# Layer norms of the second block by halves on three engines, and the bias table copied from DRAM to DRAM

## The chip, the cores and the metric

The kernel runs on one core of a Trainium2 chip. The metric is the device time of one execution in microseconds, the median over several runs. The five engines are named as the profile names them: PE is TensorE (PEld its weight loads), DVE is VectorE, ACT is ScalarE, POOL is GpSimd, SP is SyncE; SPq and ACTq are the DMA queues that SyncE and ScalarE issue into.

## What is computed

Two layers of one kind (`first_block`: a feed-forward block, a mixer, a second feed-forward block), then one layer of another kind on 256 tokens of 1024 channels in float32. The last layer is:

```
def layer_norm(x, g, b):
    xf = x.astype(jnp.float32)
    mu = xf.mean(-1, keepdims=True)
    var = jnp.square(xf - mu).mean(-1, keepdims=True)
    return ((xf - mu) * lax.rsqrt(var + LN_EPS)).astype(x.dtype) * g + b

def hybrid_layer(...):
    h = x @ w_in
    ...
    attn = moba_attention(to_heads(q), to_heads(k), to_heads(v), rel_bias)
    ...
    mix = jnp.concatenate([attn, conv, pool], axis=-1) @ w_out
    x = layer_norm(DEEPNORM_ALPHA * x + mix, ln1_g, ln1_b)
    up = causal_dwconv(x @ w_up, ffn_conv_w) + ffn_conv_b
    u, g = jnp.split(up, 2, axis=-1)
    ff = (u * jax.nn.silu(g)) @ w_down
    return layer_norm(DEEPNORM_ALPHA * x + ff, ln2_g, ln2_b)
```

The attention of that layer adds a bias that depends on the distance of query and key alone: `tab[t5_bucket(rel)]` for 8 heads.

## The kernel before

The 256 tokens lie as two tiles of 128 (`x[:, t, :]`, t = 0 and 1, 1024 channels each); `HALVES` names the four pieces of 512 channels, (0,0), (0,1), (1,0), (1,1). Every engine has its program written out by hand in its own order, and semaphores (`S[...]`) tie them together. Float32 products are made of three passes with a high and a low part: weights come by DMA of 1 MB from SyncE (`fill`, L461) into six slots, ScalarE writes the high part (`act_high`, L433, the copy itself L437), VectorE the low part (`dve_low`, L439, L442), and a slot is filled again when both have read it. So a late load shows as a wait of ScalarE for the DMA, then of VectorE for ScalarE, then of TensorE for VectorE.

A feed-forward block (`pe_ffn`, `act_ffn`, `dve_ffn`) runs over 11 groups of 256 hidden channels: groups 0 and 1 written out, 2 to 9 in a loop, 10 written out. There are four of them in layers 0 and 1 (f = 0 and 1 in each), all with the same work; once a group VectorE writes `ff_lo` (L670). The bias table: early in the kernel TensorE makes one row of 384 values per head, and VectorE puts it in `spread` (8 partitions x 384). For the attention, query row p needs the row shifted by p, so the row is first written 128 times to `scratch` in DRAM, and `bias2` is then loaded from there with one element less per partition (L2075, issued by SyncE in the second block's program behind `sp.wait_ge(spread_out, 32)`). The writing is `act_bias_out` (L366), called at the end of groups 0 and 1 of the last feed-forward block of layer 1 (L654): four heads each time, 4 x 128 rows of 1536 B read from four partitions of `spread`:

```
act.dma_start(scratch.ap().rearrange("p h x -> h p x")[at],
              spread[at].unsqueeze(1).broadcast_to([4, P, 384])).then_inc(spread_out, 16)
```

The layer norms of the second block are in `dve_ln` (L1914), run twice (n = 0 behind the output projection, n = 1 at the end of the kernel). TensorE gives the four pieces of the sum in order ("half_done" for the first three, "used" for the last). VectorE adds the residual in two pieces (L1923), takes the statistics (L1928, L1930), subtracts the mean and multiplies by the gain over all 1024 channels (L1936), and scales by the reciprocal root and adds the bias (L1942). ScalarE makes the root (`act_ln`, L1907). Tile 0 and tile 1 are interleaved on VectorE: `residual(0), stats(0), centred(0), residual(1), scaled(0), stats(1), centred(1), scaled(1)`. Behind norm 0, TensorE transposes x, eight times a tile (`pe_turn`, L738), and ScalarE (L767) and VectorE (L775) write the high and low parts of the transposed x in four pieces; the first matmul of the next block waits for the third. ScalarE loads the gains and biases of norm 1 into `ln_gb` when norm 0 is done (L1874). Behind norm 1, ScalarE issues one store per token tile (L1904).

## Time and profile before

| | us |
|---|---|
| median of 3 runs | 1517.83 (1517.06 to 1518.89) |
| profiled execution, its own time | 1520.03 |
| its span in the profile | 1518.0 |
| TensorE (PE) busy | 1415.2 (93%) |
| VectorE (DVE) busy | 941.1 (62%) |
| ScalarE (ACT) busy | 716.9 (47%) |
| GpSimd (POOL) busy | 179.7 (12%) |

Busy times of engines overlap. The mean granted clock of TensorE is 0.964 of full speed, and 230.53 MB went over the DMA queues, 152 GB/s over the span. All starts are in us from the span's start.

### The profile page before, as it was taken

To read this page: it belongs to the slowest core of one execution; us is meant where nothing else is said; L and a number is where in the kernel's file an instruction comes from. 1 tells how busy PE (TensorE), PEld (TensorE's weight loads), DVE (VectorE), ACT (ScalarE), POOL (GpSimd) and SP (SyncE) were. 2 spreads that over 40 slices of the span, in tenths; PEclk is the share of its full clock that TensorE was granted. 3 is DMA by queue.
4 is the path that set the end of the run, shared out by engine and by line. 5 is a ranking of instruction groups with operands and counts; after the bars stand their busy time and mean duration, and the time that the engine had idled before them with its cause. 6 is when DMAs were issued, how large, how long until landed. Compare 5 with 4: busy or idle time off the path is not lost.

```text
span 1518.0 us, 25173 instructions
## 1 busy us (share of the span) xinstructions
PE 1415.2 (93%) x10017; PEld 1238.2 (82%) x10017; DVE 941.1 (62%) x1246; ACT 716.9 (47%) x1010; POOL 179.7 (12%) x177
## 2 busy tenths in 40 slices
PE   6999999998899999999999998896999989799995
PEld 5888889887788887888889877785888967789995
DVE  5665567666666556666666665654566554577666
ACT  6444465444644446444466444633444334344442
POOL 3000000495000000000000495000000041000000
PEclk9999999999999999999999999998999988799998
DMA  9655373101665544655373100757644720755530
GB/s 327 222 193 180 102 242 105 57 3 40 218 217 191 192 151 156 222 179 182 115 229 119 57 3 28 229 124 208 211 139 138 241 113 30 241 174 168 202 100 28
DMA packets 173163, 230.53 MB, mean 152 GB/s; under 512 B 4576, under 2 KB 154752, under 8 KB 172958
## 3 DMA queue, kind: packets, MB, share of 16 engines
q1 hardware_dynamic: 169664, 222.71, 44.4%
q10 hardware_dynamic: 2813, 6.62, 1.7%
q8 instruction: 55, 0.90, 0.2%
q0 software_dynamic: 608, 0.12, 0.0%
q14 instruction: 23, 0.18, 0.0%
HBM read 226.81 MB, written 2.62 MB: 151 GB/s over the span
## 4 chain that ended last, share of the span: by engine, by line
PE 74%; POOL 10%; DVE 7%; DMA 4%; ACT 3%; issue 2%; SPq 1%; ACTq 0%; DVEq 0%; POOLq 0%
PE bank L457 41%; PE bank L555 20%; PE bank L556 10%; POOL mix L1698 5%; POOL proj L1696 4%; DMA w_up<-in_ffn_w_up_dram 3%; DVE hT L775 1%; DVE up_lo L442 1%; DVE gate_lo L442 1%; DMA w_gate<-in_ffn_w_gate_dram 1%; PE bank L1004 1%; PE bank L1047 0%; SPq L467 0%; DVE x L710 0%; ACT up_hi L437 0%
## 5 line engine op out<-in xcount | busy, mean ns | idle before, releaser
L555 PE MATMUL bank<-hT,gate_hi 128*128 128x512 f32 x704 | 259.7, 409 | 15.6 <-DVE gate_lo L442 10.0
L555 PE MATMUL bank<-hT,up_hi 128*128 128x512 f32 x704 | 252.1, 400 | 7.6 <-DVE up_lo L442 7.6
L442 DVE TENSOR_TENSOR down_lo<-w_down,down_hi 128x2048 fp32r<-128x2048 f32 x67 | 153.5, 2291 | 99.5 <-ACT down_hi L437 99.5
L442 DVE TENSOR_TENSOR gate_lo<-w_gate,gate_hi 128x2048 fp32r<-128x2048 f32 x67 | 153.5, 2290 | 81.4 <-ACT gate_hi L437 81.3
L556 PE MATMUL bank<-hT,gate_lo 128*128 128x256 f32 x704 | 201.6, 286 | 0.0
L635 ACT ACTIVATE work<-bank 128x256 f32<-128x256 f32 x176 | 66.7, 383 | 279.3 <-PE bank L556 279.3
L556 PE MATMUL bank<-hT,up_lo 128*128 128x256 f32 x704 | 198.3, 282 | 0.0
L442 DVE TENSOR_TENSOR up_lo<-w_up,up_hi 128x2048 fp32r<-128x2048 f32 x72 | 162.6, 2258 | 48.8 <-ACT up_hi L437 48.7
L437 ACT ACTIVATE down_hi<-w_down 128x2048 fp32r<-128x2048 f32 x67 | 128.3, 1916 | 109.1 <-PE bank L457 105.7
L555 PEld LDWEIGHTS bank<-hT,gate_hi 128*128 128x128 f32 x704 | 137.1, 195 | 51.6 <-issue 18.1
L555 PEld LDWEIGHTS bank<-hT,up_hi 128*128 128x128 f32 x704 | 132.9, 189 | 42.0 <-DVE up_lo L442 5.4
L437 ACT ACTIVATE up_hi<-w_up 128x2048 fp32r<-128x2048 f32 x72 | 136.5, 1896 | 58.3 <-PE bank L457 44.7
L457 PE MATMUL bank<-down_hi,ff_hi 128*128 128x512 f32 x400 | 157.8, 394 | 3.3 <-DVE down_lo L442 3.3
L457 PE MATMUL bank<-down_hi,ff_lo 128*128 128x512 f32 x400 | 156.9, 392 | 0.0
L457 PE MATMUL bank<-down_lo,ff_hi 128*128 128x512 f32 x400 | 156.6, 392 | 0.0
L679 DVE TENSOR_TENSOR work<-bank,work 128x256 f32<-128x256 f32 x176 | 73.6, 422 | 130.8 <-ACT work L635 130.8
L457 PE MATMUL bank<-hT,up_hi 128*128 128x256 f32 x768 | 144.6, 290 | 3.9 <-DVE hT L775 3.9
L437 ACT ACTIVATE gate_hi<-w_gate 128x2048 fp32r<-128x2048 f32 x67 | 128.3, 1915 | 35.6 <-PE bank L457 17.2
L556 PEld LDWEIGHTS bank<-hT,gate_lo 128*128 128x128 f32 x704 | 137.9, 196 | 1.4
L556 PEld LDWEIGHTS bank<-hT,up_lo 128*128 128x128 f32 x704 | 133.8, 190 | 0.0
L457 PEld LDWEIGHTS bank<-hT,up_hi 128*128 128x128 f32 x768 | 123.3, 198 | 6.1 <-issue 5.3
L457 PE MATMUL bank<-hT,gate_hi 128*128 128x256 f32 x608 | 113.3, 288 | 1.5 <-DVE hT L775 1.5
(322 smaller groups left out, 2422.5 us busy)
## 6 DMA issues: line engine op xcount, KB each, us to landing
w_gate<-in_ffn_w_gate_dram SPq DMA_DIRECT2D x44, 1024.0 KB, 5.4
w_up<-in_ffn_w_up_dram SPq DMA_DIRECT2D x44, 1024.0 KB, 5.4
w_down<-in_ffn_w_down_dram SPq DMA_DIRECT2D x44, 1024.0 KB, 5.0
w_up<-in_w_in_dram SPq DMA_DIRECT2D x12, 1024.0 KB, 11.0
w_down<-in_w_in_dram SPq DMA_DIRECT2D x12, 1024.0 KB, 8.4
w_gate<-in_w_up_dram SPq DMA_DIRECT2D x11, 1024.0 KB, 6.0
w_up<-in_w_up_dram SPq DMA_DIRECT2D x11, 1024.0 KB, 5.2
w_down<-in_w_down_dram SPq DMA_DIRECT2D x11, 1024.0 KB, 5.0
```

The source lines that it names most:

```text
L437: act.activation(staged[kind][0][:, 0:cols], slot[sl][:, 0:cols], ACT.Copy).then_inc(high[sl], 1)
L442: dve.tensor_tensor(staged[kind][1][:, 0:cols], slot[sl][:, 0:cols], staged[kind][0][:, 0:cols].bitcast(F32), ALU.subtract).then_inc(split ...
L457: mm = pe.matmul(out_, lhs(l_), rhs(r_), start=first and i == 0, stop=last and i == 2, **kw)
L555: pe.matmul(bank[:, :], w[0][:, c, at], hpair[:, :, c, :], start=c == 0, stop=False)
L556: mm = pe.matmul(bank[:, 0:SEQ], w[1][:, c, at], hT[0][:, c, :], start=False, stop=c == KC - 1)
L635: act.activation(low[:, q, j * SEQ:(j + 1) * SEQ], psum[2 * q + j][:, SEQ:], ACT.Copy)\
L679: dve.tensor_tensor(whole[:, q, at], psum[2 * q + j][:, 0:SEQ], low[:, q, at], ALU.add)\
L775: dve.scalar_tensor_tensor(hT[1][:, c:c + step, t * P:(t + 1) * P], turned_bank(t, c, step), col(gain, c) if gain else 1.0, hT[0][:, c:c + ...
L1004: mm = pe.matmul(out_[:, 6 * t:6 * t + 6], src(c, t), const("pick")[:, 10 - 2 * c:16 - 2 * c], start=(c == 0), stop=(c == 2))
L1696: link(pool.tensor_tensor(part[:, :, lag:], z[:, :, 0:n], per_channel("conv_dw_w", CONV_W - 1 - lag, n), mult))
L1698: ins = pool.tensor_tensor(acc[:, :, lag:], acc[:, :, lag:], part[:, :, lag:], add)
```

## The change

1. The bias table. `act_bias_row` writes the 8 x 384 values once to a new DRAM tensor `bias_row` (12 KB), in group 1 of the first feed-forward block. Four DMAs then copy this row of 3072 values 32 times each into `scratch`, from DRAM to DRAM; ScalarE issues them in groups 0 and 1 of the second feed-forward block of layer 0 and of the first one of layer 1. SyncE waits for 64 instead of 32.
2. The layer norms. VectorE takes each half through residual and statistics as it comes. Tile 0 is then normalised by ScalarE (one pass a half, with reciprocal root as scale and minus mean times it as bias) and finished by GpSimd (times gain, plus bias, a half at a time). Tile 1 stays on VectorE, the last step in halves.
3. TensorE transposes a half as soon as it is ready (`pe_turned_ln`), and the output is stored in four halves.

```
+        bias_row = nc.dram_tensor("bias_row", [NH2, 384], F32)
+        def act_bias_row(act):
+            act.wait_ge(spread_ready, 1)
+            act.dma_start(bias_row.ap(), spread).then_inc(row_out, 16)
...
         def act_bias_out(act, part):
             if part == 0:
-                act.wait_ge(spread_ready, 1)
-            at = slice(4 * part, 4 * part + 4)
-            act.dma_start(scratch.ap().rearrange("p h x -> h p x")[at],
-                          spread[at].unsqueeze(1).broadcast_to([4, P, 384])).then_inc(spread_out, 16)
+                act.wait_ge(row_out, 16)
+            row = bass.AP(bias_row, 0, [[0, 32], [1, NH2 * 384]])
+            act.dma_start(scratch.ap()[32 * part:32 * part + 32].rearrange("p h x -> p (h x)"), row)\
+               .then_inc(spread_out, 16)
...
-                if (uses.layer, f) == (DEPTH - 1, 1) and isinstance(g, int) and g < 2:
-                    act_bias_out(act, g)
+                if uses.layer + f == 0 and isinstance(g, int) and g == 1:
+                    act_bias_row(act)
+                if uses.layer + f == 1 and isinstance(g, int) and g < 2:
+                    act_bias_out(act, 2 * uses.layer + g)
...
+        def pe_turned_ln(pe):
+            for t, h in HALVES:
+                pe.wait_ge(S[("ln_pooled", "normed")[t]], h + 1 + past[("ln_pooled", "normed")[t]])
+                for c in range(4):
+                    mm = pe.transpose(psum[4 + 2 * t + h][:, c * P:(c + 1) * P],
+                                      x[:, t, h * 512 + c * P:h * 512 + (c + 1) * P], ident)
+                mm.then_inc(S["turned"], 1)
...
-            pe_turn(pe, 1, x, "normed", count=0)
+            pe_turned_ln(pe)
...
-            act.wait_ge(S["normed"], NT + past["normed"])
+            act.wait_ge(S["ln_pooled"], 2 + past["ln_pooled"])
+            act.wait_ge(S["normed"], 2 + past["normed"])
...
-            for t in range(NT):
-                act.wait_ge(S["normed"], NT + t + 1 + past["normed"])
-                act.dma_start(out[0, t * P:(t + 1) * P, :], x[:, t, :]).then_inc(stored, 16)
-            act.wait_ge(stored, 16 * NT)
+            for t, h in HALVES:
+                act.wait_ge(S[("ln_pooled", "normed")[t]], 2 + h + 1 + past[("ln_pooled", "normed")[t]])
+                act.dma_start(out[0, t * P:(t + 1) * P, h * 512:(h + 1) * 512], x[:, t, h * 512:(h + 1) * 512])\
+                   .then_inc(stored, 16)
+            act.wait_ge(stored, 16 * len(HALVES))
...
+                if t == 0:
+                    act.wait_ge(S["ln_factors"], n + 1 + past["ln_factors"])
+                    for h in range(2):
+                        xs = x[:, 0, h * 512:(h + 1) * 512]
+                        act.activation(xs, xs, ACT.Identity, bias=lnbias[:, 0:1], scale=rstd[:, 4:5])\
+                           .then_inc(S["ln_flat"], 1)
+
+        def pool_ln(pool, n):
+            pool.wait_ge(x_in, 16 * (1 + 2 * n + 2))
+            for h in range(2):
+                at = slice(h * 512, (h + 1) * 512)
+                pool.wait_ge(S["ln_flat"], 2 * n + h + 1 + past["ln_flat"])
+                pool.tensor_tensor(x[:, 0, at], x[:, 0, at], ln_gb[:, 0, at], ALU.mult).then_inc(S["ln_scaled"], 1)
+                pool.wait_ge(S["ln_scaled"], 2 * n + h + 1 + past["ln_scaled"])
+                pool.tensor_tensor(x[:, 0, at], x[:, 0, at], ln_gb[:, 1, at], ALU.add).then_inc(S["ln_pooled"], 1)
...
+            half_in(0, 0)
+            half_in(0, 1)
+            half_in(1, 0)
+            dve.wait_ge(S["rms_root"], NT * n + 1 + past["rms_root"])
+            link(dve.reciprocal(rstd[:, 4:5], rstd[:, 0:1]))
+            dve.scalar_tensor_tensor(lnbias[:, 0:1], lnvar[:, 0, 0:1], -1.0, rstd[:, 4:5], ALU.mult, ALU.mult)\
+               .then_inc(S["ln_factors"], 1)
+            half_in(1, 1)
+            dve.wait_ge(x_in, 16 * (1 + 2 * n + 2))
+            link(dve.scalar_tensor_tensor(x[:, 1, :], x[:, 1, :], lnvar[:, 1, 0:1], ln_gb[:, 0, :],
+                                          ALU.subtract, ALU.mult))
+            dve.wait_ge(S["rms_root"], NT * n + 2 + past["rms_root"])
+            link(dve.reciprocal(rstd[:, 5:6], rstd[:, 1:2]))
+            for h in range(2):
+                at = slice(h * 512, (h + 1) * 512)
+                dve.scalar_tensor_tensor(x[:, 1, at], x[:, 1, at], rstd[:, 5:6], ln_gb[:, 1, at],
                                          ALU.mult, ALU.add).then_inc(S["normed"], 1)
...
-            sp.wait_ge(spread_out, 32)
+            sp.wait_ge(spread_out, 64)
```

`half_in(t, h)` is residual and statistics of one half (and the aggregate behind the second half of a tile), each step waiting for the one before. Line numbers behind the change are a few higher than before.

ScalarE's order at the bias copies, before, in group 0 of the last feed-forward block of layer 1 (`hot` holds `spread`; the sizes are those of the destination):

```order
L648 ACT_TABLE_LOAD
L648 ACTIVATE work<-work 128x512
L437 ACTIVATE up_hi<-w_up 128x2048
L437 ACTIVATE down_hi<-w_down 128x2048
L371 DMA bias_scratch<-hot 4x128x384
L635 ACTIVATE work<-bank 128x256 x2
L437 ACTIVATE gate_hi<-w_gate 128x2048
```

And after, in group 0 of the second feed-forward block of layer 0:

```order
L655 ACT_TABLE_LOAD
L655 ACTIVATE work<-work 128x512
L444 ACTIVATE up_hi<-w_up 128x2048
L444 ACTIVATE down_hi<-w_down 128x2048
L378 DMA bias_scratch<-bias_row 32x3072
L642 ACTIVATE work<-bank 128x256 x2
L444 ACTIVATE gate_hi<-w_gate 128x2048
```

The copy has the same place in a group, now in two other blocks, and its outer dimension is 32 where it was 4.

VectorE's order in the first of the two norms, before:

```order
L1923 SCALAR_TENSOR_TENSOR x<-x,bank 128x512 x2
L1928 BN_STATS small<-x 128x6 x2
L1930 BN_AGGR small<-small 128x2
L1936 SCALAR_TENSOR_TENSOR x<-x,small,work 128x1024
L1923 SCALAR_TENSOR_TENSOR x<-x,bank 128x512 x2
L1941 RECIPROCAL small<-small 128x1
L1942 SCALAR_TENSOR_TENSOR x<-x,small,work 128x1024
L1928 BN_STATS small<-x 128x6 x2
L1930 BN_AGGR small<-small 128x2
L1936 SCALAR_TENSOR_TENSOR x<-x,small,work 128x1024
L1941 RECIPROCAL small<-small 128x1
L1942 SCALAR_TENSOR_TENSOR x<-x,small,work 128x1024
```

And after, from the third half on (`work` is the gain and bias, `bank` the sum in PSUM):

```order
L1956 SCALAR_TENSOR_TENSOR x<-x,bank 128x512
L1957 BN_STATS small<-x 128x6
L1967 RECIPROCAL small<-small 128x1
L1968 SCALAR_TENSOR_TENSOR small<-small 128x1
L1956 SCALAR_TENSOR_TENSOR x<-x,bank 128x512
L1957 BN_STATS small<-x 128x6
L1960 BN_AGGR small<-small 128x2
L1972 SCALAR_TENSOR_TENSOR x<-x,small,work 128x1024
L1975 RECIPROCAL small<-small 128x1
L1978 SCALAR_TENSOR_TENSOR x<-x,small,work 128x512 x2
```

Two of the four passes over 1024 channels with `work` as input are gone from VectorE. What they did stands at the end of GpSimd's program, for both norms behind its last step of the pooling:

```order
L2081 TENSOR_TENSOR work<-work,proj 128x512
L1944 TENSOR_TENSOR x<-x,work 128x512
L1946 TENSOR_TENSOR x<-x,work 128x512
L1944 TENSOR_TENSOR x<-x,work 128x512
L1946 TENSOR_TENSOR x<-x,work 128x512
```

The four operations on x come once for each norm, after ScalarE's two passes L1936.

## Rows read from the trace of the kernel before

**Rows 1.** The page, part 4: the chain that ended last, by engine

```profile
PE 74%; POOL 10%; DVE 7%; DMA 4%; ACT 3%; issue 2%; SPq 1%; ACTq 0%; DVEq 0%; POOLq 0%
```

**Rows 2.** Line L670, last blocks of layer 0, layer 1: min/median/max ns, starts

```profile
L670 DVE TENSOR_TENSOR ff_lo<-work,ff_hi x10: 692/693/694, 411.9 to 557.5; 128x512 fp32r<-128x512 f32 x10
...
L670 DVE TENSOR_TENSOR ff_lo<-work,ff_hi x10: 691/693/694, 982.8 to 1145.5; 128x512 fp32r<-128x512 f32 x10
```

**Rows 3.** Waits of TensorE, 930 to 1200 us: total us, times, longest

```profile
PE bank L555 <- DVE gate_lo L442: 10.0, 1, 10.0
PE bank L555 <- DVE up_lo L442: 4.6, 3, 2.1
```

**Rows 4.** Timeline of SyncE's queue and ScalarE: start us, duration us

```profile
407.53 0.37 SPq L467 DMA_DIRECT2D w_gate<-in_ffn_w_gate_dram  x1
...
997.85 20.04 SPq L467 DMA_DIRECT2D w_up<-in_ffn_w_up_dram  x1
...
414.68 1.93 ACT L437 ACTIVATE gate_hi<-w_gate 128x2048 fp32r<-128x2048 f32 x1
```

**Rows 5.** Windows, last block of layer 1; last columns: TensorE clock, DMA share, GB/s

```profile
1003.00:1006.00 3.00, 3.00 (x19) 2.58 (x18) 1.42 (x2) 2.36 (x3) 0.00 (x0) 1.00 0.25 41
...
1036.00:1039.00 3.00, 0.00 (x0) 0.00 (x0) 0.00 (x0) 1.10 (x1) 0.00 (x0) 0.50 0.26 38
```

**Rows 6.** DMA issues: page part 6 (KB, us to landing); the bias load L2075

```profile
w_gate<-in_ffn_w_gate_dram SPq DMA_DIRECT2D x44, 1024.0 KB, 5.4
...
L2075 SPq DMA_DIRECT2D work<-bias_scratch x1: 1534/1534/1534, 1191.0 to 1191.0; - x1
```

**Rows 7.** Timeline around the first norm: start us, duration us

```profile
1279.39 0.63 ACT L856 ACTIVATE hT<-mix 128x512 fp32r<-128x512 f32 x1
...
1290.80 1.28 DVE L1923 SCALAR_TENSOR_TENSOR x<-x,bank 128x512 f32<-128x512 f32 x2
...
1292.12 1.29 DVE L1928 BATCH_NORM_STATS2 small<-x 128x6 f32<-128x512 f32 x2
1293.44 0.21 DVE L1930 BATCH_NORM_AGGREGATE small<-small 128x2 f32<-128x12 f32 x1
...
1295.41 0.28 ACT L1911 ACTIVATE small<-small 128x1 f32<-128x1 f32 x1
1296.32 0.16 DVE L1941 RECIPROCAL small<-small 128x1 f32<-128x1 f32 x1
...
1300.80 1.29 DVE L1942 SCALAR_TENSOR_TENSOR x<-x,small,work 128x1024 f32<-128x1024 f32 x1
...
1302.14 1.97 PE L746 MATMUL bank<-cst,x 128*128 128x128 f32 x8 [2.31 <-DVE x L1942]
...
1305.65 0.77 PE L457 MATMUL bank<-hT,gate_hi 128*128 128x256 f32 x2 [1.54 <-DVE hT L775]
...
1311.93 0.40 PE L457 MATMUL bank<-hT,gate_hi 128*128 128x256 f32 x2
```

**Rows 8.** Timeline where GpSimd and VectorE work on SBUF at once

```profile
285.67 1.23 POOL L1684 TENSOR_TENSOR proj<-proj 128x512 f32<-128x512 f32 x1 [272.89 <-ACT proj L1397]
...
914.78 3.05 POOL L1696 TENSOR_TENSOR proj<-proj,par 128x464 f32<-128x464 f32 x1
...
919.26 0.95 POOL L1696 TENSOR_TENSOR proj<-proj,par 128x462 f32<-128x462 f32 x1
...
914.72 2.29 DVE L442 TENSOR_TENSOR down_lo<-w_down,down_hi 128x2048 fp32r<-128x2048 f32 x1 [0.31 <-ACT down_hi L437]
...
903.12 2.71 DVE L1626 TENSOR_TENSOR work<-work,cst 128x384 f32<-128x384 f32 x2
```

**Rows 9.** The second norm: timeline of VectorE, and the stores L1904

```profile
1504.22 0.69 DVE L1923 SCALAR_TENSOR_TENSOR x<-x,bank 128x512 f32<-128x512 f32 x1 [0.74 <-PE bank L457]
...
1513.63 1.28 DVE L1942 SCALAR_TENSOR_TENSOR x<-x,small,work 128x1024 f32<-128x1024 f32 x1
...
L1904 ACTq DMA_DIRECT2D out_dram<-x x2: 344/344/345, 1512.1 to 1514.9; - x2
```

More of the change, by code:

```diff
@@ L176 @@
     "cl_ready": 1, "mixc_ready": 2, "pool_ready": 0, "pool_mm": 0, "taps_act": 0, "taps_picked": 0, "lag_done": 0,
-    "taps_done": 0, "stats_ready": 0,
+    "taps_done": 0, "stats_ready": 0, "ln_factors": 0, "ln_flat": 0, "ln_scaled": 0, "ln_pooled": 0,
 }
@@ L208, in build @@
         spread_out = ctx.enter_context(nc.semaphore("spread_out"))
+        row_out = ctx.enter_context(nc.semaphore("row_out"))
         bias_in = ctx.enter_context(nc.semaphore("bias_in"))
@@ L223, in build @@
             mixa_ready conv_sig conv_acc cl_mean cl_sq cl_var cl_root cl_ready mixc_ready
-            pool_ready pool_mm taps_act taps_picked lag_done taps_done stats_ready""".split()
+            pool_ready pool_mm taps_act taps_picked lag_done taps_done stats_ready ln_factors ln_flat ln_scaled ln_pooled""".split()
         S = {n: ctx.enter_context(nc.semaphore(n)) for n in names}
@@ L1912, in act_ln @@
                    .then_inc(S["rms_root"], 1)
-        def dve_ln(dve, uses, kind, n, link):
-            def residual(t):
-                for h in range(2):
-                    if (t, h) != HALVES[-1]:
-                        dve.wait_ge(S["half_done"], 3 * n + 2 * t + h + 1 + past["half_done"])
-                    else:
-                        products_done(dve, uses, kind, -1)
-                    xs = x[:, t, h * 512:(h + 1) * 512]
-                    ins = dve.scalar_tensor_tensor(xs, xs, ALPHA, psum[4 + 2 * t + h][:, :], ALU.mult, ALU.add)
-                link(ins)
-            def stats(t):
-                for h in range(2):
-                    ins = dve.bn_stats(lnstat[:, h, :], x[:, t, h * 512:(h + 1) * 512])
-                link(ins)
-                dve.bn_aggr(lnvar[:, t, :], lnstat).then_inc(S["stats_ready"], 1)
-                dve.wait_ge(S["stats_ready"], NT * n + t + 1 + past["stats_ready"])
-            def centred(t):
-                if t == 0:
-                    dve.wait_ge(x_in, 16 * (1 + 2 * n + 2))
-                link(dve.scalar_tensor_tensor(x[:, t, :], x[:, t, :], lnvar[:, t, 0:1], ln_gb[:, 0, :],
-                                              ALU.subtract, ALU.mult))
-            def scaled(t):
-                dve.wait_ge(S["rms_root"], NT * n + t + 1 + past["rms_root"])
-                link(dve.reciprocal(rstd[:, 4 + t:5 + t], rstd[:, t:t + 1]))
-                dve.scalar_tensor_tensor(x[:, t, :], x[:, t, :], rstd[:, 4 + t:5 + t], ln_gb[:, 1, :],
-                                         ALU.mult, ALU.add).then_inc(S["normed"], 1)
-            residual(0)
-            stats(0)
-            centred(0)
-            residual(1)
-            scaled(0)
-            stats(1)
-            centred(1)
-            scaled(1)
@@ new lines, in dve_ln, with half_in @@
+        def dve_ln(dve, uses, kind, n, link):
+            def half_in(t, h):
+                if (t, h) != HALVES[-1]:
+                    dve.wait_ge(S["half_done"], 3 * n + 2 * t + h + 1 + past["half_done"])
+                else:
+                    products_done(dve, uses, kind, -1)
+                xs = x[:, t, h * 512:(h + 1) * 512]
+                link(dve.scalar_tensor_tensor(xs, xs, ALPHA, psum[4 + 2 * t + h][:, :], ALU.mult, ALU.add))
+                ins = dve.bn_stats(lnstat[:, h, :], xs)
+                if h == 1:
+                    link(ins)
+                    dve.bn_aggr(lnvar[:, t, :], lnstat).then_inc(S["stats_ready"], 1)
+                    dve.wait_ge(S["stats_ready"], NT * n + t + 1 + past["stats_ready"])
+            half_in(0, 0)
[14 more added lines that the diff above has]
+                dve.scalar_tensor_tensor(x[:, 1, at], x[:, 1, at], rstd[:, 5:6], ln_gb[:, 1, at],
+                                         ALU.mult, ALU.add).then_inc(S["normed"], 1)
@@ L2054, in pool_second @@
             pool.tensor_tensor(u, v, p_, ALU.subtract).then_inc(S["pool_ready"], 1)
+            pool_ln(pool, 0)
+            pool_ln(pool, 1)
         @block.sync
```

## Prediction

> **What bounds the kernel now.** I read the page first. TensorE carries 74% of the chain that ended last [rows 1], so a change pays only where TensorE stands still, or where it makes TensorE wait anew. The change touches three stretches of time: a feed-forward block whose first two groups also issue the bias copies, and the two layer norms of the second block.
>
> First the copies. A plain comparison sizes them. All feed-forward blocks of layers 0 and 1 do the same work, and VectorE's write of ff_lo (L670) comes once a group. Its ten occurrences span 411.9 to 557.5 us in layer 0, which is 145.6 us, and 982.8 to 1145.5 us in layer 1, which is 162.7 us [rows 2]. Both runs of ten start before a stall can act, so the last block loses **17.1 us**. The waits of TensorE name the place: one of 10.0 us for gate_lo and three of 4.6 us together for up_lo [rows 3]. Behind those stands a weight load, and the issue rows show why. SyncE hung in one issue for 20.04 us from 997.85, where an issue takes 0.37 us in layer 0 [rows 4]. The window rows tell what kept the queues busy: from 1003 to 1006 the DMA engines are busy for 0.25 of their time at 41 GB/s, and from 1036 to 1039 still for 0.26 at 38 GB/s, with TensorE idle and its granted clock at 0.50, the 1.2 GHz level [rows 5]. A quarter of 16 engines is four, and the copy has four outer rows. The other twelve engines idle, but a weight load is whole only when its share on the four slow ones has landed. The return to 2.4 GHz after that pause lies inside the 17.1 us.
>
> **The change, part by part.** *The old copies go.* Their 17.1 us go with them: in that block nothing else delays TensorE, as the twin block shows. What is late next there is what is late in layer 0, the usual low_copied and silu steps, which are in the 145.6 us already.
>
> *Four new copies come*, of 32 rows of 12,288 B (393 KB) each, in groups 0 and 1 of the two feed-forward blocks before. No row shows a transfer from DRAM to DRAM, so I bound it. Above: the old copy ran at 41 GB/s over four engines, 10 GB/s each; 393 KB over 16 engines is 24.6 KB each, 2.4 us. Below: nothing. The cover is the time between a load's landing and its use: in layer 0's group 0 a gate load is issued at 407.53, such a load lands in 5.4 us, and ScalarE takes it up at 414.68 [rows 4, 6], 1.75 us later than it could. Beyond that cover each copy costs at most 2.4 - 1.75 = 0.65 us, 2.6 us for four. I take **+0.3 us**, near the lower end, since TensorE is not ScalarE and stands further behind. Their issues, and that of the 12 KB row copy in the first block, stand in ScalarE's program between work that waits for TensorE anyway; at the 0.37 us of an issue they hide there, and without that wait each would cost its 0.37. The wait of SyncE for 64 instead of 32 stands ahead of the bias load at 1191.0 us [rows 6], more than 500 us behind the last copy, so neither it nor the loads behind it move.
>
> *The layer norms.* Before, VectorE does all of it. In the first one it starts at 1290.80, ends at 1302.09 (1300.80 + 1.29), and TensorE's first matmul of the next block starts at 1305.65 [rows 7]. After, VectorE takes each half as it comes: 0.68 us for the residual and 0.68 for the statistics, with two gaps of 0.02, is 1.41 us a half. Three halves and one aggregate (0.24) end at 1295.27. ScalarE's root is there at 1295.69, as before [rows 7]. The reciprocal and the one-column factor, 0.19 each, end at 1296.06. ScalarE's first pass over 512 elements (0.63 as in hT<-mix) hands over at about 1296.7, and GpSimd starts at 1296.83.
>
> Here comes the point I was not sure of. A GpSimd tensor_tensor with two full inputs over 512 elements takes 1.23 us. But beside a VectorE tensor_tensor with both inputs in SBUF the two exclude each other: GpSimd's L1696 takes 3.05 us instead of 0.95 while VectorE's L442 runs, ending 0.82 us behind it; and two VectorE operations L1626 of 384 elements take 2.71 us beside GpSimd [rows 8]. VectorE's centring and scaling read x and a gain or bias row, both in SBUF. So from the handover on I let them take turns: GpSimd 1.23 for the first, then 1.23 - 0.13 = 1.10 for each that was already waiting (0.95 - 0.82 = 0.13 is what passes before it needs the port); VectorE 1.2 for centring, 0.6 for each scaled half. From 1296.83: 1298.06, centring 1299.26, add 1300.36, scaled 1300.96, multiply 1302.06, scaled 1302.66, add **1303.76**. Before, all was normalised at 1302.09. Then TensorE turns the second half of token tile 0 and the first of tile 1 at 0.98 us for four transposes (1.97 for eight), to 1305.7, and ScalarE's and VectorE's third piece, 0.6 to 0.7 each, follow: TensorE starts at 1307.1 instead of 1305.65, **+1.5 us**. The clock does not change this: before, two matmuls of 256 columns take 0.77 us at 1305.65 and 0.40 from 1311.93 on, so they start at the lower level already.
>
> The second norm has no PE behind it, only the stores. The second half is given by TensorE at 1504.22 [rows 9]. 1.41 + 0.24, a third half of 1.41, the factors 0.37 and ScalarE's 0.63 bring the handover to 1508.35 and GpSimd's start to 1508.4. The same turns, 6.93 us, end at 1515.33. Then three stores are still to be issued at 0.34 us each, the last one at 1516.1. Before, the last issue at 1514.9, behind VectorE's last scaling (1513.63 + 1.28), ended the span at 1518.0, 3.05 us later [rows 9]; so the end comes at 1519.1, **+1.1 us**. Half-size stores can be a little quicker.
>
> **Sum.** -17.1 + 0.3 + 1.5 + 1.1 = -14.2 us. The profiled execution took 1520.03 us for a span of 1518.0, 2.2 us above the median of 1517.83, so its own time would become 1505.8 and its span 1503.8; the predicted median is 1517.83 - 14.2 = **1503.6 us**.
>
> **A rule of the Trainium skill.** Rows 8 show tensor_tensor alone; no row has a scalar_tensor_tensor with two SBUF inputs beside GpSimd, and I took it for the same. The Trainium skill, "SBUF — State Buffer", section "Who interferes with whom", states that any VectorE instruction with two SBUF inputs contends with a GpSimd instruction that reads SBUF; by it the turns hold and the sum is 1503.6, without it rival A's 1500.2. For the copies, "DMA: Bandwidth & Descriptors", section "Why a DMA increments its semaphore by 16 and not by 1", states that a transfer uses the largest number of engines up to 16 that divides the outer dimension of both sides: 4 for the old one, with which the trace agrees (0.25), and 16 for 32 rows, which no run here shows yet.
>
> **The rivals.** *A: no turns.* scalar_tensor_tensor leaves GpSimd alone. For it: no row shows this operation beside GpSimd. Against it: the tensor_tensor of [rows 8], with the same two SBUF inputs. GpSimd then needs 4 x (1.23 + 0.08) = 5.2 us: 1302.1 in the first norm (-0.1 us for TensorE, behind the transposes) and 1513.65 in the second (-0.7). The time is 1517.83 - 17.1 + 0.3 - 0.8 = 1500.2.
>
> *B: the new copies still hold loads back.* For it: a cover of 1.75 us is short, and an unknown kind of transfer could take longer than 2.4. Against it: TensorE's own distance [rows 4, 6]. If half of the old stall came back, 8.5 us, the time is 1512.
>
> *C: slower.* The copies from DRAM to DRAM land on few engines. The old pair held four engines for 2 x 786 KB / 41 GB/s = 38.4 us and cost 17.1, so 21.3 us were absorbed. If the new ones ran on two engines, each copy would hold them for 196.6 KB at 10.25 GB/s, 19.2 us, a pair again 38.4, and the 17.1 us would come twice: 1517.83 + 17.1 + 2.6 = 1537.5. It decides from a pair's 21.3 us on, below 3.7 engines. Against it: the four outer rows on four engines [rows 5], where the new form has 32.
>
> **How the numbers follow.** Forecast 0.75, A 0.15, B 0.06, C 0.04. The forecast's own range is 1501 to 1507: copies 0 to 2.6, norms 1 to 4 us. The range of 8 in 10 reaches down to A and ends at 1507: 1499.5 to 1507.0. A measurement of this kernel can tell 0.2%, 3 us, from no change. Faster is the forecast, A and B but for a little of it: 0.95; same 0.01; slower 0.04.
>
> **What would show it.** Right, step by step: L670's counterpart spans 146 us in layer 1's last block, and no wait of 10 us for gate_lo stands in it; SyncE's issues there are 0.4 to 2 us long; the DMA share beside each new copy is well above 0.25 for 2 us or less; the two earlier blocks keep 145.6 within 1 us; GpSimd's eight operations of 512 elements in the norms show 1.2 to 2.4 us, those with the wait inside the long ones; TensorE's first matmul behind the norm comes 16 us or so from VectorE's first residual instead of 14.85; the last store is issued after GpSimd's last add. Wrong: a share of 0.13 or 0.06 for tens of us behind a copy (C), a wait for up_lo or gate_lo in the two earlier blocks (B), or GpSimd operations all near 1.25 us (A).

## The result and the profile after

| | before | after |
|---|---|---|
| median | 1518.01 us (1517.06 to 1518.89, 4 runs) | 1506.04 us (1504.69 to 1507.55, 4 runs) |
| ratio, 95% interval | 1 | 0.9921, 0.9904 to 0.9939 |
| profiled execution, its own time | 1520.03 us | 1504.9 us |
| span | 1518.0 us | 1503.1 us |

The change makes the kernel 12.0 us faster, where 14.2 were forecast. The spans differ by 14.9 us. Part of that distance lies in which executions were profiled: the one before took 2.0 us more than the median of its kernel (1520.03 and 1518.01), the changed one 1.1 us less (1504.9 and 1506.04).

The page of the changed kernel, parts 1 and 4: TensorE's share of the chain that ended last is 79%, where it was 74% [rows 1].

```profile
PE 1411.7 (94%) x10017; PEld 1235.0 (82%) x10017; DVE 941.8 (63%) x1246; ACT 720.9 (48%) x1014; POOL 193.5 (13%) x185
...
PE 79%; POOL 10%; DVE 5%; ACT 3%; issue 2%; DMA 1%; ACTq 0%; POOLq 0%; SPq 0%; DVEq 0%
```

Line L679 of the changed kernel, the counterpart of L670 [rows 2], for the blocks of layer 0 and layer 1 (min/median/max ns, first and last start):

```profile
L679 DVE TENSOR_TENSOR ff_lo<-work,ff_hi x10: 691/692/693, 411.8 to 557.4; 128x512 fp32r<-128x512 f32 x10
...
L679 DVE TENSOR_TENSOR ff_lo<-work,ff_hi x10: 691/692/693, 981.5 to 1127.1; 128x512 fp32r<-128x512 f32 x10
```

Both span 145.6 us now, so exactly the 17.1 us are gone. TensorE's waits from 930 to 1180 us name no gate_lo, and up_lo once, where [rows 3] had 10.0 and 4.6 us. SyncE's issues there, 20.04 us long at worst [rows 4], are all short:

```profile
PE bank L1311 <- POOL mix L1707: 4.3, 1, 4.3
...
PE bank L562 <- DVE up_lo L449: 1.0, 1, 1.0
```

```profile
989.68 0.37 SPq L474 DMA_DIRECT2D w_gate<-in_ffn_w_gate_dram  x1
995.60 0.37 SPq L474 DMA_DIRECT2D w_up<-in_ffn_w_up_dram  x1
```

The new copies, L378, with the row copy L371 (ns an issue, starts; the last line is from issue to landing):

```profile
L378 ACTq DMA_DIRECT2D bias_scratch<-bias_row x4: 475/487/585, 408.4 to 619.9; - x4
L371 ACTq DMA_DIRECT2D bias_row<-hot x1: 288/288/288, 49.1 to 49.1; - x1
...
DMA to landing us min/median/max: 5.2/5.6/6.1
```

The two blocks that now issue them span 145.6 us (above) and 145.5 us (ff_lo from 605.6 to 751.1): the copies cost nothing.

The first norm of the changed kernel, timeline (start us, duration us; [rows 7] is before):

```profile
1272.43 0.68 DVE L1956 SCALAR_TENSOR_TENSOR x<-x,bank 128x512 f32<-128x512 f32 x1
...
1277.74 1.52 ACT L1936 ACTIVATE x<-x,small 128x512 f32<-128x512 f32 x2 [0.42 <-DVE small L1968]
...
1278.70 1.26 POOL L1944 TENSOR_TENSOR x<-x,work 128x512 f32<-128x512 f32 x1 [39.34 <-ACT x L1936]
...
1279.32 1.73 DVE L1972 SCALAR_TENSOR_TENSOR x<-x,small,work 128x1024 f32<-128x1024 f32 x1
1280.04 2.12 POOL L1946 TENSOR_TENSOR x<-x,work 128x512 f32<-128x512 f32 x1
...
1281.28 3.10 DVE L1978 SCALAR_TENSOR_TENSOR x<-x,small,work 128x512 f32<-128x512 f32 x2
1282.12 1.71 POOL L1944 TENSOR_TENSOR x<-x,work 128x512 f32<-128x512 f32 x1
...
1283.91 1.59 POOL L1946 TENSOR_TENSOR x<-x,work 128x512 f32<-128x512 f32 x1
...
1285.55 2.82 PE L1796 MATMUL bank<-cst,x 128*128 128x128 f32 x12 [2.22 <-POOL x L1946]
...
1289.06 0.77 PE L464 MATMUL bank<-hT,gate_hi 128*128 128x256 f32 x2 [0.68 <-DVE hT L784]
```

Read the GpSimd rows from the top. The first takes 1.26 us; it begins before VectorE turns to two SBUF inputs. From 1279.32 on VectorE works on x and a gain or bias row, and GpSimd's equal operations take 2.12, 1.71 and 1.59 us, while VectorE's centring takes 1.73 instead of 1.3 us and its two halves 1.55 each instead of 0.65. The engines take turns, as forecast. The first matmul comes 16.63 us behind the first residual, where it was 14.85. TensorE had 12 transposes left behind GpSimd's last add, because its program takes piece (0,1) before the two pieces of tile 1.

The second norm of the changed kernel, timeline; [rows 9] is before:

```profile
1488.09 0.69 DVE L1956 SCALAR_TENSOR_TENSOR x<-x,bank 128x512 f32<-128x512 f32 x1 [0.45 <-PE bank L464]
...
1495.94 4.67 ACTq L1922 DMA_DIRECT2D out_dram<-x  x4
1497.66 1.59 POOL L1946 TENSOR_TENSOR x<-x,work 128x512 f32<-128x512 f32 x1
```

From the second residual to the end of the span it is 15.01 us (1503.1 - 1488.09), before 13.78.

### The profile page after: what moved, and what is told of

Its sections match the earlier page's. It is cut to its first block, busy times and chain, and to the rows that moved or that the text cites. A ratio compares the mean times of both kernels' runs of the same rounds, so it can differ in the third digit from the quotient of the medians.

```text
span 1503.1 us, 25191 instructions
## 1 busy us (share of the span) xinstructions
PE 1411.7 (94%) x10017; PEld 1235.0 (82%) x10017; DVE 941.8 (63%) x1246; ACT 720.9 (48%) x1014; POOL 193.5 (13%) x185
## 4 chain that ended last, share of the span: by engine, by line
PE 79%; POOL 10%; DVE 5%; ACT 3%; issue 2%; DMA 1%; ACTq 0%; POOLq 0%; SPq 0%; DVEq 0%
PE bank L464 44%; PE bank L562 21%; PE bank L563 11%; POOL mix L1707 5%; POOL proj L1705 4%; DVE hT L784 1%; DVE up_lo L449 1%; ACT hT L776 1%; DMA w_gate<-in_ffn_w_gate_dram 1%; PE bank L1013 1%; PE bank L1056 0%; DVE x L719 0%; ACT up_hi L444 0%; DVE work L2034 0%; POOL x L1944 0%
```

## The experiments

Each part alone, then the mechanisms, then a better order. What was expected stands as it was written before the run.

**The new copies alone**: the norms, the transposes and the stores as before.

> The new copies with the old layer norms. My theory (the old copies cost 17.1 us, the new norms give 3.0 us of it back: 1.8 in the first and 1.2 in the second by the trace of the change): 1518.0 - 17.1 + about 0.3 = 1501.2 us, some 3 us under the changed kernel, and the first norm again 14.85 us from VectorE's first residual to TensorE's first matmul. The rival, that the norms are neutral or a gain and that the missing 2 us of the forecast were lost to the copies in the two earlier blocks: as slow as the changed kernel, 1505 to 1506 us, or slower.

Measured: 1503.29 us (1500.77 to 1504.79, 4 runs), ratio 0.9897 (0.9883 to 0.9912) to the kernel before, 1518.35 us beside it. From the first residual to the first matmul it is 14.84 us, from the second residual of the second norm to the end 13.75 us: both as before. The copies bring 15.1 us. The measured time is 2.1 us above the expected one, in a spread of 4 us over the runs; in the trace 1.1 us of it lies between the first and the second residual of the second norm, which are 2.56 us apart here and 1.42 in the kernel before.

**The new norms alone**: the bias copies as before.

> The new layer norms with the old copies. My theory: slower than the kernel before by 3.0 us, 1521.0 us, with the last block of layer 1 again 162.7 us for the ten writes of ff_lo. The rival (norms a gain): 1516 us or less.

Measured: 1518.27 us (1511.92 to 1523.43, 12 runs), ratio 1.0006 (0.9989 to 1.0022). That speaks against the 3 us. In the trace, however, the two intervals are the 16.63 us and (1516.0 - 1501.03) 14.97 us of the changed kernel. What pays for them in this execution can be seen: the old stall is a little shorter,

```profile
L672 DVE TENSOR_TENSOR ff_lo<-work,ff_hi x10: 691/692/693, 982.4 to 1143.0; 128x512 fp32r<-128x512 f32 x10
```

160.6 us instead of 162.7, and TensorE's clock is back earlier behind the first norm. Its first pair of matmuls takes 0.48 instead of 0.77 us, and from the first matmul to the first residual of the second norm it is 194.52 us, where the changed kernel needs 197.16 and the one before 197.15: -2.6 us. The windows behind the first matmul (last columns: granted clock, DMA share, GB/s), first of this kernel, whose first matmul starts at 1303.95, then of the changed one, where it starts at 1289.06:

```profile
1300.00:1305.00 5.00, 3.87 (x21) 3.50 (x22) 2.95 (x5) 2.28 (x4) 0.39 (x1) 0.67 0.60 209
```

```profile
1285.00:1290.00 5.00, 3.76 (x16) 3.40 (x17) 2.84 (x5) 2.28 (x4) 0.50 (x1) 0.50 0.51 210
1290.00:1295.00 5.00, 5.00 (x35) 5.00 (x34) 1.93 (x1) 0.00 (x0) 0.00 (x0) 0.74 0.31 101
```

So the norms' price is there, and in this kernel the moment at which the clock returns hid it. Whether it always does so here, one profile cannot tell.

**The changed kernel and the new copies alone, once more side by side**, to settle whether the norms cost anything in time.

> The changed kernel itself once more, in one job with the new copies alone and with another order of the pieces. Theory (the norms cost 1.8 us in the first and 1.2 us in the second): 1506.0, 3.0 us above the copies alone. Rival (the norms cost nothing in time, as the run with the new norms alone seems to say with its ratio of 1.0006): within 1 us of the copies alone. In the trace 16.6 us from the first residual of the first norm to TensorE's first matmul behind it, 15.0 from the second residual of the second norm to the end.

> New copies with the old norms, once more. Theory: 1503.0, 3 us under the changed kernel of this job; 14.8 us from the first residual to the first matmul, 13.75 from the second residual of the second norm to the end. Rival: equal to the changed kernel within 1 us.

Measured: 1504.67 us (1498.82 to 1507.27, 6 runs) and 1502.21 us (1499.54 to 1504.32, 4 runs); ratios 0.9901 (0.988 to 0.9922) and 0.989 (0.9875 to 0.9906). The difference is 2.5 us, as it was 2.8 us between the first two measurements, but the intervals overlap. The traces don't: 16.64 against 14.85 us to the first matmul, 15.03 against 13.72 us to the end, 3.1 us together. I take the norms' price as about 3 us, shown in the traces and only likely in the times.

**No turns**: tile 1 stays in PSUM until its last step, so VectorE's operations beside GpSimd have one SBUF input less.

```
+                to = psum[6 + h][:, :] if t else xs
-                link(dve.scalar_tensor_tensor(xs, xs, ALPHA, psum[4 + 2 * t + h][:, :], ALU.mult, ALU.add))
+                link(dve.scalar_tensor_tensor(to, xs, ALPHA, psum[4 + 2 * t + h][:, :], ALU.mult, ALU.add))
```

(The centring then works in `psum[6 + h]`, in halves, and the last step reads it from there and writes x.)

> The changed kernel, but VectorE keeps tile 1 of both norms in PSUM: the residual is written over the sum in PSUM, statistics are taken and centring is done there, and the scaling writes x in SBUF. So no VectorE operation of these norms beside GpSimd has two inputs in SBUF. Theory of the turns: GpSimd's eight operations all take 1.25 us instead of 1.26 to 2.12, its last add of a norm ends 1.4 us earlier against VectorE's first residual (11.6 instead of 13.07 us), the scaled halves of VectorE take 0.7 us each instead of 3.10 for two, and the time falls by about 2.5 us against the changed kernel, to 1503.5. The rival, that GpSimd is that slow by itself or waits for ScalarE: its operations keep 1.6 to 2.1 us and the time does not move.

Measured: 1502.43 us (1499.56 to 1503.62, 4 runs), ratio 0.9894 (0.988 to 0.9909). GpSimd in the first norm of this kernel, timeline:

```profile
1278.16 1.26 POOL L1944 TENSOR_TENSOR x<-x,work 128x512 f32<-128x512 f32 x1 [39.34 <-ACT x L1936]
1279.50 1.26 POOL L1946 TENSOR_TENSOR x<-x,work 128x512 f32<-128x512 f32 x1
1280.71 1.28 POOL L1944 TENSOR_TENSOR x<-x,work 128x512 f32<-128x512 f32 x1
1282.07 1.26 POOL L1946 TENSOR_TENSOR x<-x,work 128x512 f32<-128x512 f32 x1
```

All four take the time of one alone, and VectorE's last step beside the third (two halves) is short too:

```profile
1280.43 1.41 DVE L1981 SCALAR_TENSOR_TENSOR x<-bank,small,work 128x512 f32<-128x512 f32 x2
```

That is 0.71 us a half, where it was 1.55. The first matmul comes 15.00 us behind the first residual, the end 13.43 us behind the second residual of the second norm: 1.6 us each less than in the changed kernel. So VectorE's operations with two SBUF inputs were the whole cause of the long rows. The centring's output moved to PSUM as well, so for it input and output aren't told apart; the last step still writes x in SBUF, and only its input changed.

**One copy of eight heads instead of two of four**, otherwise the kernel before.

```
-            at = slice(4 * part, 4 * part + 4)
-            act.dma_start(scratch.ap().rearrange("p h x -> h p x")[at],
-                          spread[at].unsqueeze(1).broadcast_to([4, P, 384])).then_inc(spread_out, 16)
+            at = slice(0, 8)
+            act.dma_start(scratch.ap().rearrange("p h x -> h p x")[at],
+                          spread[at].unsqueeze(1).broadcast_to([8, P, 384])).then_inc(spread_out, 16)
...
-                if (uses.layer, f) == (DEPTH - 1, 1) and isinstance(g, int) and g < 2:
+                if (uses.layer, f) == (DEPTH - 1, 1) and isinstance(g, int) and g < 1:
```

(SyncE then waits for 16.)

> The kernel before, but the bias copy is one DMA of all eight heads (outer dimension 8, the same 1024 rows of 1536 B out of SBUF) in group 0 of the same block, instead of two DMAs of four. Theory (the copy runs on as many engines as its outer dimension allows, and a load is whole only when its share on these has landed): the DMA share beside it is 0.5 at about 82 GB/s, it lasts 19 us instead of 38, which is under the 21 us that were absorbed, so nearly all of the 17.1 us goes: 1501 to 1504 us. The rival, that bytes, the small packets out of SBUF or the place in this block make the stall: still 1513 us or more, since all of these are as before.

Measured: 1502.28 us (1500.56 to 1503.2, 4 runs), ratio 0.9897 (0.9883 to 0.9911). The windows beside the copy, and ff_lo in the last block:

```profile
1003.00:1006.00 3.00, 3.00 (x18) 2.56 (x17) 1.79 (x3) 0.63 (x2) 0.00 (x0) 1.00 0.52 81
```

```profile
L670 DVE TENSOR_TENSOR ff_lo<-work,ff_hi x10: 692/692/693, 979.6 to 1125.2; 128x512 fp32r<-128x512 f32 x10
```

Half of the engines at 81 GB/s, 10 GB/s each as before [rows 5], and no stall: 145.6 us. The run changes two things at once, the number of engines and, with one issue in group 0, the moment of the second half. Either way the same 1.57 MB are moved by twice the engines, which at 81 GB/s takes 19.4 us instead of 38.4. The whole gain of the bias part was to be had by these few words, without a second DRAM tensor.

**The new copies in the old place**: two in each of groups 0 and 1 of the last feed-forward block of layer 1.

```
-                if uses.layer + f == 1 and isinstance(g, int) and g < 2:
-                    act_bias_out(act, 2 * uses.layer + g)
+                if (uses.layer, f) == (DEPTH - 1, 1) and isinstance(g, int) and g < 2:
+                    act_bias_out(act, 2 * g)
+                    act_bias_out(act, 2 * g + 1)
```

> The changed kernel with its four copies from DRAM to DRAM put where the old ones stood, two in each of groups 0 and 1 of the last feed-forward block of layer 1. Theory (the form was at fault, not the place): all four copies together hold 16 engines for 1.57 MB, some 10 to 20 us of a share above 0.4, no wait of TensorE over 3 us in that block, time within 1.5 us of the changed kernel. Rival (the place was at fault, the last block has less slack): a wait for gate_lo comes back, 5 to 17 us, and 1511 to 1523.

Measured: 1506.16 us (1498.94 to 1507.19, 4 runs), ratio 0.9909 (0.9886 to 0.9933), and

```profile
L680 DVE TENSOR_TENSOR ff_lo<-work,ff_hi x10: 691/691/693, 981.9 to 1127.6; 128x512 fp32r<-128x512 f32 x10
```

145.7 us. The form was at fault and not the place, and the run before says that of the form the outer dimension is enough. Of the bias part of the change, the move to other blocks does nothing.

**Four, two and one engine.** The new copies with another outer dimension; in the third a fifth copy of 4 rows does the rest.

```
-            row = bass.AP(bias_row, 0, [[0, 32], [1, NH2 * 384]])
-            act.dma_start(scratch.ap()[32 * part:32 * part + 32].rearrange("p h x -> p (h x)"), row)\
+            row = bass.AP(bias_row, 0, [[0, 4], [0, 8], [1, NH2 * 384]])
+            act.dma_start(scratch.ap()[32 * part:32 * part + 32].rearrange("(a b) h x -> a b (h x)", a=4), row)\
```

> The changed kernel with each of its four DRAM to DRAM copies written as 4 x 8 rows instead of 32 rows: the same bytes, outer dimension 4 as in the old copies. Theory (the outer dimension sets how many DMA engines share a transfer): a share of 0.25 at about 41 GB/s beside each copy, for 9.6 us a copy instead of 2.4; a pair takes 19.2 us, under the 21.3 us that the old place absorbed, so no wait of 10 us and a time within 2 us of the changed kernel, 1505 to 1508. Rival (DRAM to DRAM is quick whatever its form): shares and landing times as in the changed kernel.

> The same with 2 x 16 rows. Theory: a share of 0.12 at about 20 GB/s, 19.2 us a copy, 38.4 us a pair as with the old copies, in two blocks: the ten ff_lo writes of the second block of layer 0 and of the first of layer 1 span 160 us or so instead of 145.6, SyncE hangs in an issue for 20 us in each, and the time is 1520 to 1537. Rival: the share is not set by the outer dimension and the time stays at 1505.

> The changed kernel with its copies of 31 rows of 12,288 B instead of 32 (a fifth one of 4 rows, behind the last, does the rest): 31 has no divisor up to 16 but 1. The two kernels before showed 98 GB/s at a share of 0.25 with an outer dimension of 4 and 49 GB/s at 0.12 with 2, which is 24.5 GB/s an engine, and no stall. Theory (the outer dimension sets the number of engines, and a pair of copies costs what it holds them for beyond the 21.3 us that the old pair absorbed): one engine, a share of 0.06 at 24.5 GB/s, 15.6 us a copy, 31.1 us a pair, so 9.8 us lost in each of the two blocks that issue a pair: the ten ff_lo writes span 155 us there instead of 145.6, and the time is 1524. Rival 1 (31 rows are spread over 15 or 16 engines all the same): 1505, landing in 5 us. Rival 2 (what matters is the share of the engines held, not the time): one slow engine of 16 costs little, under 5 us in all.

Measured: 1504.68 us (1502.51 to 1506.59), 1504.65 us (1500.87 to 1507.54) and 1506.82 us (1502.13 to 1507.26), 4 runs each; ratios 0.9906 (0.9889 to 0.9923), 0.9917 (0.9894 to 0.994) and 0.9922 (0.9896 to 0.9948). One window of each, of four, two and 31 outer rows, where only the engines of the copy are busy (in the last one they also carry what is left of the loads):

```profile
413.00:415.00 2.00, 1.06 (x7) 0.69 (x6) 2.00 (x2) 2.00 (x4) 0.00 (x0) 1.00 0.23 98
```

```profile
410.50:413.00 2.50, 1.45 (x9) 1.01 (x8) 2.50 (x2) 2.50 (x4) 0.00 (x0) 1.00 0.12 49
```

```profile
440.00:445.00 5.00, 5.00 (x27) 4.25 (x26) 2.83 (x3) 1.92 (x1) 0.00 (x0) 1.00 0.06 27
```

Shares of four, two and one sixteenth of the engines: the outer dimension sets how many take part. But an engine moves 24.5 GB/s here (98 / 4, 49 / 2) where it moved 10 before, so two engines hold a copy for 8.0 us and not 19.2. And even one engine, 31 us a pair, costs nothing, which I had not expected: ff_lo spans 145.6 and 145.7 us in the two blocks. The loads show why. A gate load of that kernel in the first of the two blocks:

```profile
L477 SPq DMA_DIRECT2D w_gate<-in_ffn_w_gate_dram x1: 3996/3996/3996, 419.6 to 419.6; - x1
...
DMA to landing us min/median/max: 29.0/29.0/29.0
```

```profile
448.64 1.92 ACT L447 ACTIVATE gate_hi<-w_gate 128x2048 fp32r<-128x2048 f32 x1
```

It lands at 448.6, and ScalarE takes it up at 448.64, in its usual place and with no idle time: just in time. In the second of the two blocks the like load lands after 29.9 us, and ScalarE waits 0.84 us for it; TensorE loses nothing there either. The same for the kernel before, in its last block:

```profile
L467 SPq DMA_DIRECT2D w_gate<-in_ffn_w_gate_dram x1: 6623/6623/6623, 991.0 to 991.0; - x1
...
DMA to landing us min/median/max: 46.9/46.9/46.9
```

```profile
1037.90 1.91 ACT L437 ACTIVATE gate_hi<-w_gate 128x2048 fp32r<-128x2048 f32 x1 [14.31 <-DMA w_gate<-in_ffn_w_gate_dram]
```

A gate load issued there is used 29.0 us later (in the changed kernel issued at 419.99, used at 448.98), and this one lands 17.9 us behind that. It would be easy to take these 17.9 us for the 17.1 us of the stall, but two covers lie between. ScalarE stands idle for 14.31 us in this row, TensorE for 10.0 [rows 3]: 4.3 us are absorbed between the two. The loads of w_up show the same, in the kernel before and in the one with a single copy of eight heads:

```profile
1016.50 1.92 ACT L437 ACTIVATE up_hi<-w_up 128x2048 fp32r<-128x2048 f32 x1 [7.16 <-DMA w_up<-in_ffn_w_up_dram]
```

```profile
1010.50 1.92 ACT L437 ACTIVATE up_hi<-w_up 128x2048 fp32r<-128x2048 f32 x1 [4.23 <-DMA w_up<-in_ffn_w_up_dram]
```

Before, TensorE then waits 1.4 us. With eight engines it waits no more in this block than in the changed kernel (1.0 us for up_lo), although ScalarE stood idle for 4.23 us; the gate load, issued at 988.23, lands after 27.6 us, at 1015.8, and is used at 1016.79. So a load that lands late at ScalarE costs nothing for its first 4 to 6 us (7.16 - 1.4, 14.31 - 10.0, and all of 4.23), and TensorE pays the rest. The stall is made of several such rests: TensorE's waits for gate_lo and up_lo are 13.6 us more than in the changed kernel (10.0 + 4.6 - 1.0), and the remaining 3.5 us are not waits; behind the two longest ones TensorE works at a lower clock, granted 0.50 from 1040 to 1045 and 0.72 from 1050 to 1055:

```profile
1040.00:1045.00 5.00, 2.72 (x8) 2.33 (x9) 4.62 (x6) 0.87 (x3) 0.00 (x0) 0.50 0.66 184
```

**The pieces in the order in which they get ready**: (0,0), (1,0), (1,1), (0,1) for transposes, high and low parts and stores, with tile 1 in PSUM. The matmuls of the first four channel blocks wait for two pieces, the others for all four.

```
+        LN_ORDER = ((0, 0), (1, 0), (1, 1), (0, 1))
...
-            for t, h in HALVES:
+            for t, h in LN_ORDER:
...
-            pe.wait_ge(S["h_low"], (2 * KC * n + KC + c + 1 if gained else 4 * n + 2 + c // 4 + 1) + past["h_low"])
+            in_four = 2 * (c // 4) + 2 if n == 1 else 2 + c // 4 + 1
+            pe.wait_ge(S["h_low"], (2 * KC * n + KC + c + 1 if gained else 4 * n + in_four) + past["h_low"])
```

> The changed kernel with token tile 1 kept in PSUM until its last step (no turns) and the pieces taken in the order in which they get ready: (0,0), (1,0), (1,1), (0,1) for transposes, high and low parts and stores; the first matmul needs only the first two. Theory: the piece (0,1) from GpSimd is the last at 11.4 us from the first residual and nothing waits for it but its own transposes, so TensorE's first matmul comes 12.2 us behind the first residual instead of 14.8 with the old norms (-2.6); in the second norm one store instead of three is left behind GpSimd's last add, 12.4 us from the second residual to the end instead of 13.75 (-1.3). 3.9 us under the copies alone, about 1499.3. Rival: the early start comes at TensorE's lower clock level and is given back in the matmuls that follow, and VectorE's and ScalarE's weight parts, now later than the matmul, make it wait: no more than 1 us under the copies alone.

> The changed kernel with the pieces in the order (0,0), (1,0), (1,1), (0,1), tile 1 in SBUF as it is there, so that GpSimd and VectorE still hinder each other. Theory: piece (1,0) is done about 10.4 us behind the first residual and the first matmul comes 3.15 us behind it as in the kernel with both, at 13.6 us (16.6 in the changed kernel, 12.4 with both); 13.3 us from the second residual of the second norm to the end. Together 4.7 us under the changed kernel: 1501. If the early start also brings the higher clock level back earlier, as it did with both, 2 us more: 1499.

The second is the changed kernel with the order alone, tile 1 in SBUF. Measured: 1494.07 us (1492.79 to 1497.46, 4 runs), ratio 0.985 (0.9833 to 0.9867), for both; 1499.74 us (1495.97 to 1501.33, 4 runs), ratio 0.9882 (0.9864 to 0.9899), for the order alone. From the first residual to the first matmul it is 12.40 and 13.56 us, from the second residual of the second norm to the end 12.0 and 13.7 us, near what was expected. What came on top is the clock. The windows behind the first matmul of the kernel with both, which starts at 1282.32:

```profile
1280.00:1285.00 5.00, 5.00 (x31) 4.69 (x30) 3.86 (x5) 2.39 (x4) 1.30 (x2) 0.67 0.43 141
1285.00:1290.00 5.00, 5.00 (x44) 5.00 (x43) 1.11 (x1) 1.16 (x1) 0.00 (x0) 1.00 0.86 288
```

and of the new copies alone, where it starts at 1289.73:

```profile
1290.00:1295.00 5.00, 5.00 (x25) 5.00 (x25) 2.38 (x2) 0.00 (x0) 0.00 (x0) 0.50 0.30 77
1295.00:1300.00 5.00, 5.00 (x40) 5.00 (x40) 0.00 (x0) 1.48 (x1) 0.00 (x0) 0.91 0.96 360
```

The one works at 2.4 GHz from about 1 us behind its first matmul on, the other over 5 us at 1.2 GHz. From there to the first residual of the second norm the one needs 194.91, the other 197.27 us. With 2.4 us for the earlier start, 2.4 for the clock and 1.7 at the end, 6.5 of the 8.1 us between the medians are found; the rest is in the scatter. That the clock's 2.4 us belong to the new order is not shown. The kernel with two engines has the norms of the changed kernel, with their 16.63 us from first residual to first matmul, and its profiled execution shows the same early return:

```profile
1288.07 0.48 PE L464 MATMUL bank<-hT,gate_hi 128*128 128x256 f32 x2 [0.68 <-DVE hT L784]
```

It needs 194.56 us to the next norm, where the five other profiled executions with these norms and new copies need 196.3 to 197.2. So the same program behind the same pause comes out either way. Both kernels with the new order have the early return, and none of the five profiled executions of the other kernels whose first matmul comes 14.8 to 15.0 us behind the residual has it, but each was profiled once. The 4.1 us of start and end are the order's and PSUM's. This kernel beats both: 10 to 12 us under the changed one, 24.2 under the one before.

## Why the prediction was right, and where not

*The old copies, -17.1 us: exact.* The last block fell from 162.7 to 145.6 us. That four engines were busy while a load waited for its share on them fits every run: with eight, in the same place, the stall is gone. On which engine a packet ran no row shows; the shares and the landings say it together.

*The new copies, +0.3 us: right in size, by wrong steps, and so by luck.* They cost 0. I bounded a copy by 10 GB/s an engine, the only rate in the rows; the new form moves 24.5, so 16 engines would need 1.0 us and not 2.4 (from the smaller counts; at 16 the copy runs beside a load and can't be told apart). And I put a gate load issued at 407.53 beside the gate_hi at 414.68 and read a cover of 1.75 us. They don't belong together: with two slots for each weight that load is for the group after, and between issue and use lie about 25 to 29 us, of which a landing takes 5 to 6. The cover is some 20 us, and TensorE stands another 4 to 6 us behind ScalarE.

*The first norm, +1.5 us: measured 1.8 (16.63 - 14.85).* The last add ends 13.07 us behind the first residual; 12.96 were forecast. Within that, GpSimd starts 6.27 us behind the first residual and not 6.03, mostly because ScalarE's pass takes 0.76 us and not 0.63 (I had taken the row of a plain copy, without columns as scale and bias); the turns were a little cheaper than I made them (6.80 us from GpSimd's first start to its last end, against 6.93). Behind the last add TensorE stands 3.56 us and not 3.34.

*The second norm, +1.1 us: measured 1.2 (15.01 - 13.78).* Turns and stores came as worked out. (The terms given for GpSimd's start add up to 1508.28 and not 1508.35, which moves nothing.)

*The sum.* -17.1 + 0 + 1.8 + 1.2 = -14.1, and the spans differ by 14.9; the other 0.8 us is where the clock happened to be low: the kernel before has a stretch from 775 to 790 us with a granted clock of 0.91, 0.50 and 0.91 in its three windows of 5 us, the changed one stays at 1.00 there and starts the last block 1.3 us earlier, but has 0.5 us more in the pieces of the last sum. The medians differ by 12.0 to 13.6 us (two measurements of the changed kernel). Runs of the changed kernel lie between 1498.8 and 1507.6, so this difference from the 14.2 can't be resolved into causes; a part of the scatter is the return of the clock behind the first norm, worth 2.6 us in the kernel with two engines. With this scatter it is partly luck that the median of 1506.04 lies under the 1507.0 at which the range ends: two of its four runs, 1507.17 and 1507.55, lie above.

*The rivals.* A (no turns) is excluded by the 2.12, 1.71 and 1.59 us, and its distance of 3.4 us from the forecast was about right: without turns the two norms gave back 1.6 us each in the trace. Its own working would have put them 0.1 and 0.7 us under the old norms; they came 0.15 above and 0.35 under. B didn't occur. C, the slower case, had the wrong price. I let a pair of copies absorb 21.3 us of 38.4 and charged the rest one for one. Two engines, for which I had said 1537.5, gave 1504.65, and one engine, 31 us a pair, still 1506.8 where the same reasoning, with the rate mended, said 1524. The loss is not a fixed part of the time for which engines are held. It is zero as long as loads land within their cover: landings of 27.8 and 29.9 us, 4.23 and 0.84 us too late for ScalarE, cost nothing. Those of 30.7 us (w_up, 7.16 us too late) and 46.9 us (w_gate, 14.31) did; between the last two no run lies. C's threshold, 3.7 engines (its own numbers give 3.6), is refuted by one and two engines without a loss, and the upper end of the range would have held with them too (1506.82 and 1504.65). C's premise of 10 GB/s an engine failed with it: a pair of copies on two engines holds them for 16 us and not 38.4.

*The Trainium skill.* On the number of engines (the Trainium skill, "DMA: Bandwidth & Descriptors", section "Why a DMA increments its semaphore by 16 and not by 1") the runs agree at every count that could be seen alone: shares of 0.52, 0.23, 0.12 and 0.06 for outer dimensions of 8, 4, 2 and 31. On two SBUF inputs beside GpSimd (the Trainium skill, "SBUF — State Buffer", section "Who interferes with whom") they agree too: 2.12, 1.71 and 1.59 us with two, 1.26 to 1.28 with one.

## What to carry to other kernels

Of a prefetched load, find the instruction that really uses it (count the slots), and compare its distance from the issue with the landing, then add what the bottleneck engine stands behind that instruction: that is the cover. A transfer that holds a few engines costs nothing while landings stay within it, and beyond it only the excess, plus what TensorE loses at the lower clock behind the wait. Give a DMA an outer dimension that 16, or at least 8, divides, before moving it elsewhere. When work is split over engines, let the consumers take the pieces in the order in which they get ready: here that and PSUM for one operand turned a loss of 3 us into a gain of 8, of which 4.1 us are found in the two norms and 2.4 in a return of the clock that may be chance.

## What the runs showed of the hardware that I had not expected

- A DMA engine moved 10 GB/s with rows of 1536 B from SBUF partitions (41 GB/s on four, 81 on eight) and 24.5 GB/s with rows of 12,288 B from DRAM (98 on four, 49 on two). Whether the length or the source makes the difference wasn't tried.
- One VectorE input in PSUM instead of SBUF takes GpSimd's 512-element operation from 1.6 to 2.1 us to 1.26, and VectorE's own from 1.55 to 0.71.
- With equal work, the return of TensorE's clock behind the first norm comes in one of two ways: about 194.5 to 194.9 us to the next norm, or 196.3 to 197.3. The early one was seen behind 12.40 and 13.56 us from first residual to first matmul, and twice behind 16.63 us (the new norms alone, and two engines); the late one behind 14.8 to 15.0 us and in five more executions behind 16.6 us. So the length of the pause doesn't decide alone. What does is open.
